# A one-core encoder layer: LayerNorms that centre x before the root is there, and affines and mean shifts moved between engines

## What is computed

```python
x = _layernorm(x, ln_in_g, ln_in_b)
h = x * (1.0 + scale[:, 0]) + shift[:, 0]
y = _swiglu(h, ffn1_w_in, ffn1_w_out)          # 1024 -> 2 x 2816 -> 1024
x = _layernorm(ALPHA * x + 0.5 * gate[:, 0] * y, post_ln_g[0], post_ln_b[0])
h = x * (1.0 + scale[:, 1]) + shift[:, 1]
cq, ckv, k_rope_raw, u = jnp.split(h @ w_in, split_at, axis=-1)
attn = _mla(cq, ckv, k_rope_raw, ...)          # RMS norms, 8 heads, chunk-causal softmax
pooled = _multiscale_pool(u, ...)              # trailing means over 2, 4, 8, 16 tokens
y = jnp.concatenate([attn, pooled], -1) @ w_out
x = _layernorm(ALPHA * x + gate[:, 1] * y, post_ln_g[1], post_ln_b[1])
h = x * (1.0 + scale[:, 2]) + shift[:, 2]
y = _swiglu(h, ffn2_w_in, ffn2_w_out)
x = _layernorm(ALPHA * x + 0.5 * gate[:, 2] * y, post_ln_g[2], post_ln_b[2])
```

## Time and profile before

| | us |
|---|---|
| median of 3 runs (1017.79 to 1018.68) | 1018.22 |
| the profiled execution | 1017.21 |
| its span | 1015.4 |

### The profile page before, as it was taken

How to read it: one execution, slowest core, us unless ns; L and a number is a source line. 1 busy time by engine, 2 the same in 40 slices (tenths; PEclk the granted TensorE clock), 3 DMA queues, 4 the chain that set the end, 5 groups by cost and what they waited for, 6 DMA issues and landing times.

```text
span 1015.4 us, 10613 instructions
## 1 busy us (share of the span) xinstructions
PE 959.9 (95%) x4130; PEld 761.6 (75%) x4130; DVE 533.2 (53%) x728; ACT 369.6 (36%) x538; POOL 244.9 (24%) x206
## 2 busy tenths in 40 slices
PE   3999999999999999989999997999999999999991
PEld 3788888888878886767667774788888888788870
DVE  5946766445638654967555387942232232233315
ACT  4732322332213314664465336433233233212214
POOL 0021111111107211557732162721111111052210
PEclk8999999999999999989999998999999999999996
DMA  9746665565454643113411011142322322223202
GB/s 369 310 136 195 188 197 196 187 197 194 160 180 142 228 143 114 42 63 104 124 42 42 21 63 63 42 151 98 104 89 98 104 91 91 94 78 108 63 16 83
DMA packets 37474, 127.20 MB, mean 125 GB/s; under 512 B 4016, under 2 KB 4144, under 8 KB 37424
## 3 DMA queue, kind: packets, MB, share of 16 engines
q1 hardware_dynamic: 37424, 126.52, 37.5%
HBM read 123.36 MB, written 2.10 MB: 124 GB/s over the span
## 4 chain that ended last, share of the span: by engine, by line
PE 83%; DVE 11%; ACT 3%; issue 2%; POOL 1%; DMA 0%; SPq 0%; ACTq 0%; DVEq 0%
PE bank L540 25%; PE bank L541 25%; PE bank L542 25%; DVE w_lo L919 2%; DVE x L1262 2%; PE bank L840 2%; PE bank L817 1%; DVE x L1256 1%; ACT w_hi L911 1%; POOL x L1645 1%; DVE lat L1278 1%; DVE x L1598 1%; PE bank L828 1%; DVE bn L1418 0%; PE bank L611 0%
## 5 line engine op out<-in xcount | busy, mean ns | idle before, releaser
L919 DVE TENSOR_TENSOR w_lo<-raw,w_hi 128x1024 fp32r<-128x1024 f32 x159 | 213.0, 1346 | 302.8 <-ACT w_hi L911 302.5
L540 PE MATMUL bank<-h_hi,w_hi 128*128 128x512 f32 x730 | 287.1, 393 | 1.8 <-DVE w_lo L919 1.8
L542 PE MATMUL bank<-h_hi,w_lo 128*128 128x512 f32 x730 | 284.5, 390 | 0.0
L541 PE MATMUL bank<-h_lo,w_hi 128*128 128x512 f32 x730 | 284.3, 389 | 0.0
L911 ACT ACTIVATE w_hi<-raw 128x1024 fp32r<-128x1024 f32 x159 | 162.2, 1031 | 204.3 <-PE bank L542 204.1
L540 PEld LDWEIGHTS bank<-h_hi,w_hi 128*128 128x128 f32 x730 | 137.2, 188 | 32.1 <-DVE w_lo L919 2.2
L1651 POOL TENSOR_TENSOR a_lo<-act_t,a_hi 128x512 fp32r<-128x512 f32 x44 | 58.8, 1339 | 419.2 <-ACT a_hi L994 419.2
L542 PEld LDWEIGHTS bank<-h_hi,w_lo 128*128 128x128 f32 x730 | 137.2, 188 | 28.8
L541 PEld LDWEIGHTS bank<-h_lo,w_hi 128*128 128x128 f32 x730 | 137.2, 188 | 28.5 <-issue 0.7
L540 PE MATMUL bank<-a_hi,w_hi 128*128 128x512 f32 x352 | 141.1, 401 | 0.0
L542 PE MATMUL bank<-a_hi,w_lo 128*128 128x512 f32 x352 | 139.5, 396 | 0.0
(11 more groups left out here) (246 smaller groups left out, 1032.3 us busy)
## 6 DMA issues: line engine op xcount, KB each, us to landing
raw<-wunits SPq DMA_DIRECT2D x145, 512.0 KB, 3.2
ada_ring<-ada_w SPq DMA_DIRECT2D x56, 512.0 KB, 4.4
ada_first<-ada_w SPq DMA_DIRECT2D x16, 512.0 KB, 9.8
raw<-wunits SPq DMA_DIRECT2D x16, 384.0 KB, 2.9
x<-xT SPq DMA_DIRECT2D x4, 512.0 KB, 5.8
outT<-x SPq DMA_DIRECT2D x8, 256.0 KB, 2.0
K<-k_rope SPq DMA_DIRECT2D x2, 512.0 KB, 7.9
c_act<-c_rows SPq DMA_DIRECT2D x1, 512.0 KB, 7.8
```

Source lines behind the costliest of these rows:

```text
L540: mm(out, lh, rh, start=first, stop=False)
L541: mm(out, lh, rl, start=False, stop=False)
L542: return mm(out, ll, rh, start=False, stop=last)
L919: nc.vector.tensor_tensor(lo, raw[:, slot, 0:width], hi.bitcast(F32), SUB).then_inc(s_lo, 1)
```

## The change

- In `root` ACT also copies the mean to `shift` (a positive mean now), and DVE subtracts it from tiles 0 to 2 while it waits for ACT's Ln and Exp (`centre`). The Newton step writes rstd into the PSUM bank `SQR[p]`, in place of an SBUF tile; `shift = -mean * rstd` is gone. `normalise` multiplies tiles 0 to 2, then centres (mean read from PSUM) and multiplies tile by tile. `opened` and its counterpart before FFN2 first add shift times the column sum (whose sign is turned in `sel`), then multiply. Both RMS norms keep rstd in PSUM too. PE has new waits for the time that these banks are in use.
- The affine of norm 1 moves from POOL, behind `hn_lo`, to ACT, in attention steps 4 to 11.
- The mixer's shift: the mean of tile 0 is taken on PE at step 16, when its pooled half is in, copied by DVE at step 17, and subtracted by POOL in steps 18 to 30. `mixer_shifted` and the mean matmul in the output projection are gone.
- DVE's weight splits in attention move from steps 0, 6, .. to steps 2, 8, .. and within the step behind its other work; ACT's halves stay. The split of `U_KNOPE` on ACT and DVE moves ahead of the RMS root of q.
- The last affine: ACT keeps tiles 0, 2, 3, 5, 7, POOL takes 1, 4, 6.

```diff
--- before.py
+++ after.py
 FILL_STEP = [3 * i // 2 for i in range(2 * len(FILL))]
+SHIFT_STEP = FILL_STEP[2 * FILL.index("p0") + 1] + 3
+SHIFTED_AFTER = {18: 0, 19: 1, 20: 4, 21: 5, 22: 6, 23: 7, 27: 2, 30: 3}
+AFFINE_STEP = 4
+POOL_LAST = (1, 4, 6)
...
             for m in range(KD):
-                sp.wait_ge(s_hh[3], m + 1)
+                if m in POOL_LAST:
+                    sp.wait_ge(s_pf, POOL_LAST.index(m) + 1)
+                else:
+                    sp.wait_ge(s_hh[3], m + 1 - sum(n < m for n in POOL_LAST))
                 sp.dma_start(outT[m], x[:, m, :]).then_inc(s_out, 16)
...
                     elif j == 0 and t == 3:
-                        pe.wait_ge(s_rv[2], 5)
+                        pe.wait_ge(s_un[2], OPEN)
...
                 if p == 2:
-                    pe.wait_ge(s_er, SPLIT_TILES)
+                    pe.wait_ge(s_e[2], SPLIT_TILES)
...
                                 if p == 2:
+                                    pe.wait_ge(s_te, STEPS)
                                     stats_begin(p)
                                 stats_mean(p)
...
                 if g == 0:
                     pe.wait_ge(s_poolw, 16)
+                    pe.wait_ge(s_full, KKV + KQ)
...
                 if t == 5:
+                    pe.wait_ge(s_un[1], OPEN)
                     pe.wait_ge(s_msum, 1)
                     mm(bank[6][:], ones_t[:], s_sum[:], start=True, stop=True).then_inc(s_mst, 1)
...
+                    if i == FILL.index("p0") + 3:
+                        pe.wait_ge(s_cc[2], 1)
...
                 elif m >= 6:
-                    pe.wait_ge(s_er, m - 5)
+                    pe.wait_ge(s_e[2], m - 5)
                 for k in range(KD):
                     last = mm3(y_bank(2, m)[:], w(unit, k * P), h(k), k == 0, k == KD - 1)
-                    if m == 4 and k == 1:
-                        pe.wait_ge(s_te, STEPS)
-                        shift_mean(2)
...
+                if step == SHIFT_STEP:
+                    pe.wait_ge(s_pr, 1)
+                    mm(bank[SHIFT_BANK][:], ones_t[:], x[:, 0, :], start=True, stop=True).then_inc(s_cm[2], 1)
...
                 fn(tmp[:], bank[MEAN[p]][:], ACT.Square).then_inc(s_rq[p], 1)
+                fn(shift[:], bank[MEAN[p]][:], ACT.Copy).then_inc(s_mc, 1)
...
             act_hi(act, MX + 7 + LEAD)
+            act_hi(act, MX + 8 + LEAD)
             rms_root(1)
             for j in range(KQ):
                 act.wait_ge(s_full, KKV + j + 1)
                 fn(cqn_hi[:, j, :], cq[:, j, :], ACT.Copy).then_inc(s_lh, 1)
-            act_hi(act, MX + 8 + LEAD)
...
+                if AFFINE_STEP <= step < AFFINE_STEP + KD:
+                    m = step - AFFINE_STEP
+                    fn(x[:, m, :], x[:, m, :], ACT.Identity, scale=cols[:, C_LNG + KD + m:C_LNG + KD + m + 1],
+                       bias=cols[:, C_LNB + KD + m:C_LNB + KD + m + 1]).then_inc(s_res[1], 1)
...
             for m in range(KD):
-                act.wait_ge(s_nx[3], 2 * m + 2)
+                if m in POOL_LAST:
+                    continue
+                act.wait_ge(s_nx[3], m + 1)
...
                 stt(var[:], bank[SQR[p]][:], SUM_EPS, tmp[:], ADD, SUB).then_inc(s_rv[p], 1)
                 if split is not None:
                     dve_lo(dve, split)
+                dve.wait_ge(s_mc, p)
+                for m in range(3):
+                    centre(p, m, shift)
                 dve.wait_ge(s_rq[p], 3)
                 tt(tmp[:], y0[:], y0[:], MUL).then_inc(s_rv[p], 1)
                 dve.wait_ge(s_rv[p], 2)
                 stt(tmp[:], tmp[:], -0.5, var[:], MUL, MUL).then_inc(s_rv[p], 1)
                 dve.wait_ge(s_rv[p], 3)
-                stt(rstd[:], tmp[:], 1.5, y0[:], ADD, MUL).then_inc(s_rv[p], 1)
+                stt(bank[SQR[p]][:], tmp[:], 1.5, y0[:], ADD, MUL).then_inc(s_rv[p], 1)
+
+            def centre(p, m, mean):
+                tt(x[:, m, :], x[:, m, :], mean[:], SUB).then_inc(s_cen[p], 1)
+
+            def normalise(p, base=None):
+
                 dve.wait_ge(s_rv[p], 4)
-                stt(shift[:], bank[MEAN[p]][:], -1.0, rstd[:], MUL, MUL).then_inc(s_rv[p], 1)
-
-            def normalise(p, base=None):
-
-                dve.wait_ge(s_rv[p], 4)
-
-                def a(m):
-                    tt(x[:, m, :], x[:, m, :], rstd[:], MUL).then_inc(s_nx[p], 1)
-
-                def b(m):
-                    if m == 0:
-                        dve.wait_ge(s_rv[p], 5)
-                    dve.wait_ge(s_nx[p], 2 * m + 1)
-                    tt(x[:, m, :], x[:, m, :], shift[:], ADD).then_inc(s_nx[p], 1)
-
-                a(0)
                 for m in range(KD):
-                    b(m)
-                    if m + 1 < KD:
-                        a(m + 1)
+                    if m >= 3:
+                        centre(p, m, bank[MEAN[p]])
+                    dve.wait_ge(s_cen[p], m + 1)
+                    tt(x[:, m, :], x[:, m, :], bank[SQR[p]][:], MUL).then_inc(s_nx[p], 1)
                     if base is not None and m == 3:
                         dve_lo(dve, base + 1 + LEAD)
-                    if base is not None and m == 6:
+                    if base is not None and m == KD - 1:
                         dve_lo(dve, base + 2 + LEAD)
...
+            col(ts(sel[0:4, 0:1], sel[0:4, 0:1], -1.0, None, MUL))
...
-                tt(dst, bank[mix_bank(t)][rows, :], rstd[rows, :], MUL).then_inc(s_evd, 1)
+                stt(dst, shift[rows, :], wg(MX + t)[rows, :], bank[mix_bank(t)][rows, :], MUL, ADD)\
+                    .then_inc(s_evd, 1)
                 dve.wait_ge(s_evd, t + 1)
-                stt(dst, shift[rows, :], wg(MX + t)[rows, :], dst, MUL, ADD).then_inc(s_un[1], 1)
+                tt(dst, dst, bank[SQR[1]][rows, :], MUL).then_inc(s_un[1], 1)
...
             lo_after(MX + 7)
             u_out(0)
+            lo_after(MX + 8)
             rms_newton(1, bank[7][:], P / QR)
             for j in range(KQ):
-                stt(cq[:, j, :], cq[:, j, :], qg[:, j:j + 1], rstd[:], MUL, MUL).then_inc(s_full, 1)
-            lo_after(MX + 8)
+                stt(cq[:, j, :], cq[:, j, :], qg[:, j:j + 1], bank[7][:], MUL, MUL).then_inc(s_full, 1)
             u_out(1)
...
-                if step % 6 == 0 and step < 36:
+                if step % 6 == 2:
                     lo_after(S_FILL + step // 6)
+                if step == SHIFT_STEP + 1:
+                    dve.wait_ge(s_cm[2], 1)
+                    cp(shift[:], bank[SHIFT_BANK][:]).then_inc(s_cc[2], 1)
...
-                stt(x[:, m, :], y_bank(2, m)[:], gate[:, 1, m:m + 1], x[:, m, :], MUL, ADD).then_inc(s_er, 1)
-
-            def mixer_shifted(m):
-
-                dve.wait_ge(s_er, m + 1)
-                tt(x[:, m, :], x[:, m, :], shift[:], SUB).then_inc(s_e[2], 1)
-
+                stt(x[:, m, :], y_bank(2, m)[:], gate[:, 1, m:m + 1], x[:, m, :], MUL, ADD).then_inc(s_e[2], 1)
+
+            dve.wait_ge(s_xs[2], KD)
             for m in range(SPLIT_TILES):
                 mixer_residual(m)
             lo_after(S_A + 1)
-            dve.wait_ge(s_cm[2], 1)
-            cp(shift[:], bank[MEAN[2]][:]).then_inc(s_cc[2], 1)
-            dve.wait_ge(s_cc[2], 1)
-            for m in range(SPLIT_TILES):
-                mixer_shifted(m)
             for m in range(SPLIT_TILES):
                 plain_low(2, m)
             for m in range(SPLIT_TILES, KD):
                 lo_after(S_OUT + m - SPLIT_TILES)
                 mixer_residual(m)
-                mixer_shifted(m)
                 if m > SPLIT_TILES:
                     plain_low(2, m - 1)
             plain_low(2, KD - 1)
...
-                    tt(dst, bank[OPEN_BANK[2][n]][:], rstd[:], MUL).then_inc(s_evu, 1)
+                    stt(dst, shift[:], wg(F2 + n), bank[OPEN_BANK[2][n]][:], MUL, ADD).then_inc(s_evu, 1)
                     dve.wait_ge(s_evu, n + 1)
-                    stt(dst, shift[:], wg(F2 + n), dst, MUL, ADD).then_inc(s_un[2], 1)
+                    tt(dst, dst, bank[SQR[2]][:], MUL).then_inc(s_un[2], 1)
...
-                for m in range(KD):
+                for m in range(KD if p == 2 else 0):
...
+                if step in SHIFTED_AFTER:
+                    m = SHIFTED_AFTER[step]
+                    pool.wait_ge(s_cc[2], 1)
+                    pool.wait_ge(s_pr, min(m + 1, SPLIT_TILES) if m < SPLIT_TILES else 1)
+                    tt(x[:, m, :], x[:, m, :], shift[:], SUB).then_inc(s_xs[2], 1)
             sums(2)
             h_split(2)
             ffn(1, 3, a_hi2, a_lo2)
+            for m in POOL_LAST:
+                c = 3 * KD + m
+                pool.wait_ge(s_nx[3], m + 1)
+                ts(x[:, m, :], x[:, m, :], cols[:, C_LNG + c:C_LNG + c + 1],
+                   cols[:, C_LNB + c:C_LNB + c + 1], MUL, ADD).then_inc(s_pf, 1)
```

More of the change, by code:

```diff
@@ L311, in build @@
         POOL_BANK = (7, 6, 4, 7)
+        SHIFT_BANK = FILL_BANK[FILL.index("p0") % 3]
         OUT_BANK = [FILL_BANK[(len(FILL) + m) % 3] for m in range(3)] + [0, 1, 4]
@@ L373, in build @@
```

(15 more changed lines are left out.)

22 lines of the change are left out of this document (11 added, 11 removed).

## The result

| | before | after |
|---|---|---|
| median, us (4 runs each) | 1018.45 (1017.79 to 1018.81) | 993.96 (993.36 to 994.68) |
| the profiled execution | 1017.21 | 994.68 |
| its span | 1015.4 | 992.9 |

The ratio is 0.9761, with a 95% interval of 0.9749 to 0.9774: 24.5 us less, where 22.5 were forecast. The forecast was 995.7, its range 993.0 to 1001.5.

A forecast was written before the change was run, and what follows sets the result against it. PE, busy 959.9 of 1015.4 us, was taken as the bound, with time lost in waits, half clock and after its last matmul. 5.4 + 0.6 + 3.7 + 2.0 + 8.5 + 2.3 = 22.5 us less gave 995.7, range 993.0 to 1001.5.

The forecast's parts named there:

- Middle affine, 5.4 us: Middle stage: with eight affines off POOL, PE's 4.0 us wait for s_sum and the half clock behind it go; 5.4 us.
- hn_lo, 0.6: Norm after FFN1: ends some 8 us earlier, so hn_lo is ahead of PE and its wait goes; 0.6 us.
- Weight splits, 3.7: First K unit and seventh FFN2 unit: both waits for w_lo go, by earlier split and shorter norm; 3.7 us.
- Attention, 2.0: Attention: 3.0 us of waits for ScalarE go, 1.0 comes back for eight affines on ScalarE; 2.0 us.
- POOL's eight subtractions: Attention: placed after a step's normalisation, their results used three steps on, so no cost; bound 1 us.
- End of the mixer, 8.5: Mixer's sums: copy and subtractions leave the chain, so PE's 6.0 us q_sum wait and half clock nearly go; 8.5 us.
- The tie: Mixer's sums: the sum is ready and PE asks at the same 607.8; 0.3 us of wait left.
- Rival A: The sums still end the wait at the mixer: 1000.7 or 1002.9 us; chance 0.12.
- Last norm, 2.3: Last norm: multiplications with PSUM input replace the steps from shift on, 10.68 us becoming 8.36; 2.3 us.
- Rival B: Attention is bound by ScalarE, all eight affines land on the path: 1003.0 us; chance 0.12.
- D: Slower: PE waits a little at every attention step and the clock falls for the stage's rest: 1020.5 us; chance 0.02.
- rival C: More than forecast: no attention cost, no mixer wait, none of the small waits left standing: 993.9 us; chance 0.07.

The follow-up runs named there:

- a_affine_pool: The changed kernel with the middle affine back on POOL behind hn_lo, none on ScalarE in attention: 992.71 us.
- b_affine_act: The kernel before with only the middle affine moved to ScalarE in attention steps 4 to 11: 1017.62 us, ratio to before 0.9999.
- a_rstd_sbuf: The changed kernel with rstd of every norm in an SBUF tile and the mean taken from the SBUF copy: 1000.64 us.
- a_knope_last: The changed kernel with the U_KNOPE split behind q's RMS root again and all of the last affine on ScalarE: 995.34 us.
- a_split_old: The changed kernel with DVE's attention splits in steps 0, 6, 12 .. as before: 995.36 us.
- a_shift_dve: The changed kernel with the mixer's eight subtractions on DVE in the output projection, none on POOL; mean and copy stay in attention: 1000.95 us.

## Why the prediction was right, and where it was not

**Middle affine, 5.4 us: the wait went, but the cause was wrong and the clock's part too small.** The wait of 4.0 us and the half clock are gone (up to 445.85 of the trace before PE's starts gained 7.1 us: 0.6 of hn_lo, 4.1 of the wait, 2.3 of the clock). The clock's 1.2 us in the term was half of what it cost: the earlier trace rows stop at 443.40, and the low level went on to 445.8, as the window of before shows.

```profile
441.00:445.80 4.80, 4.80 (x9) 3.16 (x10) 2.06 (x2) 4.78 (x8) 1.28 (x1) 0.50 0.06 11
```

But the step said that they go because the eight affines leave POOL. a_affine_pool has them back and does not wait; b_affine_act has them gone and gains nothing. The prediction looked at what ended the wait, and named in the same breath that "the norm ahead of it gets shorter". It did not ask whether that alone was enough, nor what DVE's own lateness would be with the wait gone. The unmade step is: for each engine that PE needs in the next 15 us, how late is it without the others?

**hn_lo, 0.6, and the norm's length: right.** PSUM forms take 0.685 us in the mean of all norms, where 0.69 was taken, and the step that writes rstd into PSUM 0.70 (980.44 in the kernel after). Norm 1 ends 7.4 us earlier, where some 8 were forecast. a_rstd_sbuf is 6.7 us slower, more than the prediction ever put on this (it counted some 2 us as at stake): the late norm showed itself in the w_lo, q_sum and u waits, not at hn_lo.

**Weight splits, 3.7: right in size.** Middle part 1.8 (a_knope_last undoes it for 1.8) and FFN2 2.4 where 1.9 stood. The middle stage gave 9.4 where 7.8 stood: 1.2 are the second half of the low clock (above), and some 0.6 a gap behind U_KNOPE (at 479.81 before) that the prediction had let stand; 0.3 were lost between.

**Attention, 2.0: wrong, -0.7.** With the mean's two passes, 0.9 us that the output projection gives back, it is +0.2. Three parts of the term: 3.0 of waits gone (a_split_old has 2.6 of them back in the list, 3.1 between starts: right); 1.0 for the affines on ScalarE, at the values (1.09 in a_affine_pool: right, the place too); and "POOL's eight subtractions .. I take nothing (bound: 1 us)": wrong, 1.0 us at 541.45, and likewise 0.6 at 497.19 for a split moved beside POOL's low part. 3.1 - 1.1 - 1.0 - 0.6 = 0.4, near the measured 0.2. The prediction had the rule and the row for it, and used both for the norm; it did not hold the moved splits against POOL's list. The rule of the Trainium skill (SBUF — State Buffer, "Who interferes with whom") covers it: a DVE instruction with two SBUF inputs and a GpSimd instruction that reads SBUF shut each other out. The trace agrees, with 2.37 us in place of 1.23, 1.14 longer beside a POOL instruction of 1.29, and with 1.66 in place of 0.77 for POOL's affine.

**End of the mixer, 8.5: right.** Measured 6.12 + 2.66 = 8.78. The tie that the prediction saw was one: in the kernel after POOL's last addition ends at 599.88 and PE takes it at 600.15.

```profile
598.58 1.30 POOL L1681 TENSOR_TENSOR q_sum<-q_sum,sq 128x512 f32<-128x512 f32 x1
...
599.91 0.40 PE L551 MATMUL bank<-lat,w_lo 128*128 128x512 f32 x1
...
600.15 1.02 PE L634 MATMUL bank<-s_sum,ones_d 128*128 128x512 f32 x2
```

It fell on the good side by 0.27 us, which is luck: the prediction's own two times were equal, and it had left 0.3 us of wait. a_shift_dve shows what undoing the subtractions' move costs, 5.97 + 1.69. Rival A was nearer than its chance of 0.12 says.

**Last norm, 2.3: 2.9.** The count of steps was right, their price not: for a step with a PSUM input 0.68 us was taken, from the residuals of the earlier trace rows, which are another operation. The TENSOR_TENSOR steps follow one another in 0.61 us, in after with PSUM as in before with SBUF, and in 0.72 where one needs the other's result: 7.80 us from first to last multiplication, not 8.36. Of the Trainium skill's figures (Perfetto Trace Analysis, "Optimizing Scalar/DVE Operations"), 125 ns of access against 60, these rows show nothing: 1.88 us for three steps with PSUM, 1.90 with SBUF.

Rival B (ScalarE bound in attention) did not come: the affines cost 1.1 us there, where B had all 6.5. D neither: the clock stayed at 1.00 from 60 us to the last norm. D's argument that the clock had not fallen after a wait of 2.0 us was a misreading: in the trace before PE waits 2.01 us up to 26.19, and its clock is 0.50 behind that.

```profile
26.20:29.30 3.10, 3.10 (x7) 2.42 (x8) 3.06 (x6) 3.07 (x6) 0.00 (x0) 0.50 1.01 406
```

The measured 993.96 is the time of rival C (993.9), but not by C's way: C had no cost in attention, where the affines and the slowed splits took 2.7 us.
